# Mixer trips of a hybrid attention and RWKV layer: masking a quarter of each product bank first, and moving turned rows, bonus and the last value products into the steps of the state chain

## The reference

```python
def step(S, inp):
    r_t, w_t, k_t, v_t, kk_t, akk_t = inp
    sa = jnp.einsum('zbhij,zbhj->zbhi', S, kk_t)
    S = S * w_t[..., None, :] - sa[..., :, None] * akk_t[..., None, :] + v_t[..., :, None] * k_t[..., None, :]
    return S, jnp.einsum('zbhij,zbhj->zbhi', S, r_t)
...
_, ys = lax.scan(step, S0, xs)          # 512 steps, z = 2 directions, 8 heads of 64
...
coef = jnp.einsum('bthn,zbthn,hn->bth', heads(r), heads(k_dir), r_k)
bonus = (coef[..., None] * heads(v)).reshape(B, T, C)
return ((yn + bonus) * g).astype(p.dtype)
```

## Time and profile before

| | us |
|---|---|
| median of 3 runs (1734.31 to 1736.79) | 1736.51 |
| the profiled execution | 1735.64 |
| its span, first to last instruction | 1733.5 |
| mixer, four trips (from the first X product) | 182.4 to about 460 |
| PE, DVE, ACT busy over the span | 94%, 85%, 64% |

### The profile page before, as it was taken

One profiled execution on the slowest core, in us unless ns is written; L12 is line 12 of the kernel. 1 busy time (PEld: TensorE's weight loads), 2 busy tenths in 40 slices (PEclk: granted clock), 3 DMA queues, 4 the chain that ended last, 5 costly groups with the idle time before them and its releaser, 6 DMA issues.

```text
span 1733.5 us, 33793 instructions
## 1 busy us (share of the span) xinstructions
PE 1637.6 (94%) x12579; PEld 1331.7 (77%) x12580; DVE 1478.0 (85%) x1721; ACT 1103.7 (64%) x1078; POOL 214.2 (12%) x134
## 2 busy tenths in 40 slices
PE   7999899889896999999999999999999999999993
PEld 6778787778675778888888888888888888888882
DVE  5585677676586899999999999999999999999995
ACT  4533425333325777777777777777777777777772
POOL 0001111010103121111211111111211112111110
PEclk9999989999797999999999999999999999999997
DMA  6231101000338999999999999999999999999993
GB/s 200 73 101 55 30 15 30 9 21 15 104 133 279 373 386 365 383 380 378 373 359 385 375 383 372 372 376 375 380 361 376 377 377 375 361 378 377 380 368 111
DMA packets 207631, 473.33 MB, mean 273 GB/s; under 512 B 18701, under 2 KB 29403, under 8 KB 207355
## 3 DMA queue, kind: packets, MB, share of 16 engines
q1 hardware_dynamic: 197179, 442.74, 69.2%
q0 software_dynamic: 9792, 27.28, 7.1%
q10 hardware_dynamic: 576, 2.10, 0.3%
HBM read 454.35 MB, written 26.08 MB: 277 GB/s over the span
## 4 chain that ended last, share of the span: by engine, by line
PE 60%; DMA 4%; DVE 2%; issue 1%; ACT 1%; SPq 0%; DVEq 0%; POOLq 0%; ACTq 0%
PE bank L2183 19%; PE bank L2186 19%; PE bank L2184 18%; PE bank L2209 3%; DMA w_raw<-in_expert_w_up 2%; PE bank L2193 1%; DVE moe_w_lo L2169 1%; ACT moe_w_hi L2165 0%; DMA x<-sum_rows 0%; DMA moe_x_gathered<-hn_rows,moe_gather_rows 0%; DMA sum_rows<-moe_y,moe_scatter_rows 0%; DVE x L2663 0%; DVE moe_x_lo L2220 0%; PE bank L2201 0%; DVE moe_a_lo L2220 0%
## 5 line engine op out<-in xcount | busy, mean ns | idle before, releaser
L2169 DVE TENSOR_TENSOR moe_w_lo<-w_raw,moe_w_hi 128x2048 fp32r<-128x2048 f32 x384 | 867.9, 2287 | 46.7 <-ACT moe_w_hi L2165 45.2
L2165 ACT ACTIVATE moe_w_hi<-w_raw 128x2048 fp32r<-128x2048 f32 x384 | 735.9, 1917 | 124.7 <-PE bank L2186 109.2
L2183 PE MATMUL bank<-moe_w_hi,moe_x_hi 128*128 128x512 f32 x1024 | 406.0, 396 | 0.3 <-DVE moe_w_lo L2169 0.3
L2186 PE MATMUL bank<-moe_w_lo,moe_x_hi 128*128 128x512 f32 x1024 | 400.2, 391 | 0.0
L2184 PE MATMUL bank<-moe_w_hi,moe_x_lo 128*128 128x512 f32 x1024 | 399.6, 390 | 0.0
L2186 PEld LDWEIGHTS bank<-moe_w_lo,moe_x_hi 128*128 128x128 f32 x1024 | 192.6, 188 | 41.0
L2183 PEld LDWEIGHTS bank<-moe_w_hi,moe_x_hi 128*128 128x128 f32 x1024 | 192.7, 188 | 40.2 <-DVE moe_x_lo L2220 1.3
L2184 PEld LDWEIGHTS bank<-moe_w_hi,moe_x_lo 128*128 128x128 f32 x1024 | 192.9, 188 | 38.6
L2183 PE MATMUL bank<-moe_w_hi,moe_a_hi 128*128 128x512 f32 x512 | 208.2, 407 | 1.4 <-DVE moe_a_lo L2220 1.4
L2186 PE MATMUL bank<-moe_w_lo,moe_a_hi 128*128 128x512 f32 x512 | 201.0, 393 | 0.0
L2184 PE MATMUL bank<-moe_w_hi,moe_a_lo 128*128 128x512 f32 x512 | 200.3, 391 | 0.0
(11 more groups left out here) (343 smaller groups left out, 2078.8 us busy)
## 6 DMA issues: line engine op xcount, KB each, us to landing
w_raw<-in_expert_w_up SPq DMA_DIRECT2D x512, 512.0 KB, 8.1
w_raw<-in_expert_w_down SPq DMA_DIRECT2D x256, 512.0 KB, 9.4
proj_w_raw<-in_w_in SPq DMA_DIRECT2D x36, 384.0 KB, 3.3
mixer_bias_table<-in_att_bias SPq DMA_DIRECT2D x16, 256.0 KB, 2.7
x<-in_w_o SPq DMA_DIRECT2D x8, 512.0 KB, 6.6
sum_rows<-x SPq DMA_DIRECT2D x5, 512.0 KB, 4.0
x<-in_x ACTq DMA_DIRECT2D x4, 512.0 KB, 6.7
x<-in_x SPq DMA_DIRECT2D x4, 512.0 KB, 4.0
```

Of the source, the lines that this page charges most:

```text
L2165: act.activation(w_hi[:, j % RING, :], raw[:, j % RAW, :], ACT.Copy).then_inc(hi_w[j % RING], 1)
L2169: eng.tensor_tensor(w_lo[:, j % RING, :], raw[:, j % RAW, :], w_hi[:, j % RING, :].bitcast(F32), ALU.subtract)\
L2183: pe.matmul(out, s_hi[:, k, :], w_hi[:, j % RING, w], start=first, stop=False)
L2186: ins = pe.matmul(out, s_hi[:, k, :], w_lo[:, j % RING, w], start=False, stop=ends)
```

## The change

1. **Mask.** The constant `scmask` has the first level's block pattern in its inverse quarter. DVE first takes only that quarter of each X bank, straight into `X[g]` (`first_level`, 8 operations of 128x128), adds the identity (`with_identity`), and takes the other three quarters later (`other_scores`, 8 operations of 128x384). L1363 goes. A bank is freed by `other_scores`.
2. **Banks and PE order of the front.** NT(g) moves to bank 2g, behind X(0,0) and X(1,0). PE runs X, NT(0), T(1,0), NT(1), T(1,1), the first products of level 2, then `lora` and the turned `AD` rows N(z,2), then the second products of level 2.
3. **Into the chain.** The next trip's N(z,0), N(z,1) (turned `QR` and `KD`), the next bonus K, and `values(3)` of this trip are cut into halves and quarters and stand in the chain's steps (`between`): K in steps 0 and 1, `values(3)` in 2 and 3, N in 4 to 7. Each piece stands once ahead of the wait for `sa_done` and once at the step's end. All use bank 5. ACT copies them there, ahead of Y.
4. **First trip.** Its N(z,0), N(z,1) and K are made ahead of the X products, in a set of banks of their own (`B0`), and PE waits for all their copies before the X products.
5. **DVE.** `prepare(0)` moves from before the adds of level 2 to behind `biased(0)`, next to `prepare(1)`. `weighted(3)` moves from before L1403 into the chain, behind step 3.

```diff
     for g in range(2):
-        use(("NT", g), g)
-    for z in range(2):
-        for a in range(3):
-            use(("N", z, a), 2 + 3 * z + a)
-    use(("K",), 2)
-    for g in range(2):
+        use(("NT", g), 2 * g)
         use(("T", 1, g), 2 * g + 1)
...
+    for z in range(2):
+        use(("N", z, 2), 6 + z)
...
-    use(("aO", NPAIR - 1), 7)
...
     use(("Y",), 4)
+    use(("K",), 5)
+    use(("aO", NPAIR - 1), 5)
+    for a in range(2):
+        for z in range(2):
+            use(("N", z, a), 5)
...
+                else:
+                    for key in first_keys:
+                        pe.wait_ge(B0.free_sem(key), B0.before(0, key))
+                        if key[0] == "N":
+                            ins = turn_prepared(0, key[1], key[2], B0.tile(key), range(NT))
+                        else:
+                            ins = bonus(B0.tile(key), range(NT))
+                        ins.then_inc(B0.fill_sem(key), 1)
+                    for key in first_keys:
+                        pe.wait_ge(B0.free_sem(key), B0.after(0, key))
...
-                turn(1)
-                if nxt:
-                    lora(B, it, it + 1)
+                for g in range(2):
+                    transposed_products(g)
+                    turn(1, (g,))
+
+                def lora_and_decay_keys():
+                    if nxt:
+                        lora(B, it, it + 1)
...
+                    for z in range(2):
+                        key = ("N", z, 2)
+                        done(turn_prepared(it, z, 2, bank(key), range(NT)), key)
...
+                    if i == 0:
+                        lora_and_decay_keys()
                     for g in range(2):
                         pe.wait_ge(w1d[g], LV * it + i + 1)
...
-                values(NPAIR - 1)
                 for z in range(2):
-                    copied(("N", z, 1))
+                    turned(z, 1)
...
+                def between(n, part):
+                    if n <= 1 and nxt:
+                        key = ("K",)
+                        if n == 0 and part == 0:
+                            pe.wait_ge(csum, it + 1)
+                            bank(key)
+                        ins = bonus(B.tile(key), (2 * n + part,))
...
+                    if n in (2, 3):
+                        key = ("aO", NPAIR - 1)
+                        if n == 2 and part == 0:
+                            copied(("aT", NPAIR - 1))
+                            bank(key)
+                        ins = value_part(NPAIR - 1, B.tile(key), n - 2, part)
...
+                    if n >= 4 and nxt:
+                        a, z = divmod(n - 4, 2)
+                        key = ("N", z, a)
+                        if part == 0:
...
+                            bank(key)
+                        ins = turn_prepared(it + 1, z, a, B.tile(key), (2 * part, 2 * part + 1))
...
                     own_values(n)
+                    between(n, 0)
                     if n:
                         pe.wait_ge(sa_done, NS * it + n)
...
                     if n:
                         from_state(n)
+                    between(n, 1)
...
-                if not nxt:
+                if nxt:
+                    take_bonus(B, it, it + 1)
+                    for a in range(2):
+                        for z in range(2):
+                            take_turned(B, it, z, a)
+                else:
...
+                def first_level(q):
                     for h in range(2):
                         key = ("X", q, h)
                         dve.wait_ge(B.fill_sem(key), B.count(it, key))
-                        dve.tensor_tensor(SC[:, 2 * q:2 * q + 2, h, :], B.tile(key).rearrange("p (n k) -> p n k", n=2),
-                                          scmask.rearrange("p (n k) -> p n k", n=2), ALU.mult).then_inc(B.free_sem(key), 1)
+                        dve.tensor_tensor(X[q // 2][:, 2 * (q % 2):2 * (q % 2) + 2, h, :], pairs(B.tile(key))[:, :, 0:L],
+                                          pairs(scmask)[:, :, 0:L], ALU.mult).then_inc(x1c, 1)
...
+                first_level(0)
+                first_level(1)
+                first_level(2)
+                with_identity(0)
+                first_level(3)
+                with_identity(1)
+                other_scores(0)
+                other_scores(1)
+                transposed_masked(0)
+                transposed_masked(1)
+                other_scores(2)
+                other_scores(3)
+                before_add = [(), (2,), (3,), (5,), ()]
+                after_add = [(0, 1), (), (4,), (6,), ()]
...
                 prep(7)
-                weighted(NPAIR - 1)
                 dve.wait_ge(gcd, it + 1)
...
                     dve.wait_ge(st_done, NS * it + n + 1)
+                    if n == 3:
+                        weighted(NPAIR - 1)
...
+    for pattern in out:
+        pattern[:, 0:L] *= (s >> 1 == t >> 1) & (s != t)
```

More of the change, by code:

```diff
@@ L812, in mixer @@
         B = Banks(sem, "trip", psum, *trip_banks())
+        first_keys = [("N", z, a) for a in range(2) for z in range(2)] + [("K",)]
+        B0 = Banks(sem, "first", psum, first_keys, list(range(len(first_keys))))
         NS = NCK - 1
@@ L852, in _ @@
                 pool.sem_inc(B.freed[b], 1)
+                pool.sem_inc(B0.freed[b], 1)
             def key_products(m, z):
@@ L956, in values, with turn_prepared, bonus, turned @@
                         for hf in range(2):
-                            col = HD * heads(u)[n]
-                            ins = pe.matmul(dst[:, HD * n:HD * n + HD], pT[:, u % 2, 2 * n + hf, :],
-                                            vw[:, hf, col:col + HD], start=(hf == 0), stop=(hf == 1))
+                            ins = value_part(u, dst, n, hf)
                     done(ins, key)
+                def turn_prepared(m, z, a, dst, parts):
+                    for i in parts:
+                        t = slice(P * i, P * i + P)
+                        src = (QR[z][:, 0, t], KD[z][:, t], AD[z][:, t])[a]
+                        ins = pe.transpose(dst[:, t], src, ident[:, :])
+                    return ins
+                def bonus(dst, parts):
+                    for i in parts:
+                        ins = pe.matmul(dst[:, 2 * i:2 * i + 2], tmp[:, P * i:P * i + P], headone, start=True, stop=True)
+                    return ins
+                def turned(z, a):
+                    key = ("N", z, a)
+                    if a == 2:
+                        copied(key)
+                    elif it:
+                        pe.wait_ge(B.free_sem(key), B.after(it - 1, key))
+                    else:
+                        pe.wait_ge(B0.free_sem(key), B0.after(0, key))
                 if it:
@@ L977, in trip, with transposed_products @@
                         done(last[h], ("X", q, h))
-                for g in range(2):
+                def transposed_products(g):
                     dst = bank(("NT", g))
@@ L987, in trip, with turn @@
                     done(ins, ("NT", g))
[L988 to L1001, removed]
-                def turn(lv):
-                    for g in range(2):
+                def turn(lv, gs=(0, 1)):
+                    for g in gs:
                         if lv == 1:
@@ L1096, in trip @@
                 for z in range(2):
-                    copied(("N", z, 0))
+                    turned(z, 0)
                 dst = [bank(("V", b)) for b in range(2)]
@@ L1108, in trip @@
                 for z in range(2):
-                    copied(("N", z, 2))
+                    turned(z, 2)
                 pe.wait_ge(rqd, 2 * it + 2)
@@ L1233, in trip @@
                     sigmoids(B, it, it + 1)
+                for z in range(2):
+                    take_turned(B, it, z, 2)
                 for hf in range(2):
@@ L1348, in weighted @@
                        .then_inc(B.free_sem(key), 1)
-                for q in range(4):
+                wide = lambda ap: ap.unsqueeze(1).to_broadcast([P, 8, L])
+                pairs = lambda ap: ap.rearrange("p (n k) -> p n k", n=2)
+                def first_level(q):
                     for h in range(2):
```

78 lines of the change are left out of this document (48 added, 30 removed).

## The result

The kernel after takes 1748.9 us (median, 1744.5 to 1760.3) against 1734.4 for the kernel before on the same chip: ratio 1.0100, interval 1.008 to 1.0121. Forecast were 1736.5 and no change; the time lies above the range. The profiled execution took 1748.79 with a span of 1746.9. Its times spread more than before's, and they broadly follow the clock: 1744.5 us at a mean granted clock of 0.979, 1748.8 at 0.976, 1758.8 at 0.968, 1760.3 at 0.967, though not strictly (1747.8 at 0.973).

What follows compares the result with a forecast made beforehand. The experts hold most of the wait chain and start after the mixer, so mixer time counts one to one. Fronts +0.8, entries -2.2, pieces +1.7, between trips +0.75, clock -1.0 sum to +0.05: 1736.5 us, range 1731 to 1742.

Steps and rivals of the forecast that it cites:

- part 7: Pieces in the chain's steps: cost 0.5 us a trip for three trips, 0.2 for the last, +1.7 together.
- Part 9: Clock in the chains: added PE work ends the first chain's half clock, gaining 1.0 us; the last chain's stays.
- Rival C: Pieces at half clock: 0.9 us a slow step, 1742 with one chain falling, 1746 with two; chance 0.22.
- Parts 1 to 3: Trip's front: early mask looks like 3.5 us; PE/ACT order leaves 1.3; after the scan, second trip gains 0, third 0.7.
- Part 4: Last trip's front, without lora or preparation: gain of 1.6 us.
- Part 5: First trip: N, K and their copies ahead of X cost 3.1 us, between 2.8 and 3.5.
- Part 6: Entry into the chain: gain of 0.4 us for each of three trips and 1.0 for the last, -2.2 in all.
- Part 8: Between trips: PE issues one more piece, +0.25 us each, +0.75 for three.
- rival D: Early mask comes through if ACT does not hold PE: three fronts give 2 to 3.4 us more, 1729; chance 0.08.

Runs made afterwards that it cites:

- e8_filler: Kernel before with two unread wide products (128 rows by 512 columns, bf16) in PE's two gaps of each chain step: 1732.5 us, ratio 0.9988.
- e10_narrow_filler: Kernel before with four unread narrow products (64 rows by 64 columns, fp32) in the same two gaps of each chain step: 1733.2 us, ratio 0.9985.
- f1_turn_first: e5_late_turn with pieces reordered: turned blocks in steps 0 to 3, value products in 4 and 5, K in 6 and 7; 1733.7 us, ratio 1.0008.
- e5_late_turn: Kernel after with N(z,2) moved behind T(2) of level 2 in other banks and the scan back ahead of the adds: 1740.0 us, ratio 1.004.
- the second trace: Kernel after, unchanged, run and traced a second time: 1750.4 us, ratio 1.0097.

## Why the prediction was wrong, by its steps

**Parts 7 and 9 failed, and they are the largest part of the miss.** Together they were to give +0.7 for the chains; they gave +8.7 in one trace and +5.0 in the other (56.8 less 51.8). From the end of the projection on, the first trace misses the sum by 15.4, and 8.0 of it is here; the second by 13.3, and 4.3 is here. The fronts with the first X are 5.7 and 4.6 of the miss. At full clock part 7 was right: a chain with all pieces is 13.08 against 12.46, +0.6 for 0.5 taken, and the last 12.44. Its bounds of 0 to 1.5 were read from full-clock gaps alone. Part 9 took it that the pieces hold the clock, and no row stood behind that. K's products lay in steps 0 and 1, and with them the clock fell in seven of the twelve chains that have them there without filler, about as often as with nothing there. The one right idea in it, that filled gaps hold the clock, is borne out by e8_filler, e10_narrow_filler and f1_turn_first.

**Rival C was the mechanism**, with its price (0.9 for two pieces, measured 0.9 to 1.0) and its place, the steps at half clock. Its totals did not hold: 1742 for one chain and 1746 for two, where the profiled executions took 1747.9 with one and 1748.8 with two, since the fronts missed as well. Its chance of 0.22 was too low. Two of before's four chains were already slow in part, and a new cost that is paid at half clock alone had to be weighed with that share, not with the expectation that the clock would stay up. The Trainium skill (TensorE: Matmul & The Clock Gate, Part 1) has activity release the throttle. The runs with filler agree (granted clock 1.00 in the chains of e8_filler and e10_narrow_filler); the kernel after, busier in its chains than the kernel before (1.72 against 1.27 of 2.00 in the windows shown), does not bear it out.

**Parts 1 to 3 hold in order, and their size is 0.9 off.** I let the sigmoids start at t = 10.65, behind the table load. The load ended at 10.97, and the first sigmoid began at 11.5, since it waited for PE's `lora`; the second products followed at 14.57, not 13.65. From there to mask 3 it is 7.77, for 7.7 worked out. So second and third trip are +1.07 and +0.24 at mask 3 (0 and -0.7 forecast). That N(z,2) and the scan eat the early mask was right: e5_late_turn takes both away and gains 3.1.

**Part 4**: -0.6 in the first trace, where the clock was half from 415.7 to 419.1, and -1.7 in the second (mask 3 at 18.52), for -1.6; its "2.1 less 0.25" is a slip, since 16.15 less 13.8 is 2.35 and the 2.1 has the 0.25 off already. **Part 5**: +3.5 for 3.1; its step was right, and the first trip's own front was forecast at no change and cost 2.4 with a half-clock stretch at NT (1.47), 0.9 in the second trace without it. **Part 6**: -1.6 for -2.2, and +1.1 in the second trace, where half clock lay behind mask 3 twice (208.9 to 212.3, 359.0 to 362.5). **Part 8** missed the size: the turn is +0.65 and not +0.25. The last piece of two turned blocks holds X for 0.37 (332.04 to 332.41), and the piece before it, at 331.18, holds the outputs back: they begin 0.57 after the last SA add, for 0.35 in the kernel before.

Of rival D nothing came: ACT did hold PE.

## What to carry to other kernels

Before work is put into an engine's gaps, price it twice: at the clock at which the gap is there, and at the one at which it isn't. A piece that fits a gap at full clock (1.91 against 1.89 a step) is on the path as soon as PE runs at half clock (3.15 against 2.18), and a trace of the kernel before already tells that this happens. If filled gaps are to keep the clock up, look at what fills the first steps: the same pieces in another order were worth 5 to 6 us, with intervals that just touch.

## What the runs showed of the hardware

The granted clock fell in 23 of 41 chains whose first two steps were not filled, and stayed up in the other 18. What picks the chain stays open, and whether work ahead of the chain (`values(3)`) delays the fall: the second trace of the kernel after lost one chain where the first lost two. It is open too why K's products do not hold the clock, and why e5_late_turn and f1_turn_first, which differ in the order of the pieces, differ in it. Two kinds of filler, 512 columns of bf16 on all rows and 64 columns of fp32 on half of them, held it equally. In the kernels with filler the clock then fell right behind the mixer (458.5 to 465.4 in e10_narrow_filler, 460.6 to 464.0 in e8_filler). Work that nobody reads made a kernel faster by 0.15% (0.05 to 0.25%), which I had not expected.
